# Alternating column order in the products of three stages of a hybrid decoder layer

## What is computed

```python
def s5_branch(u, ...):
    ...
    v = jax.nn.gelu(y).astype(u.dtype) @ w_glu          # 2048 x 4096
    v1, v2 = jnp.split(v, 2, axis=-1)
    return v1 * jax.nn.sigmoid(v2), ...

def mixer(h, ...):
    proj = h @ lp['w_in']
    ...
    merged = jax.nn.sigmoid(g_a) * y_a + jax.nn.sigmoid(g_b) * y_b
    return merged @ lp['w_out'], ...                    # 2048 x 2048

def swiglu(h, w_up, w_down):
    g, v = jnp.split(h @ w_up, 2, axis=-1)              # 2048 x 11264
    return (jax.nn.silu(g) * v) @ w_down                # 5632 x 2048
```

## Time and profile before

| | |
|---|---|
| median of 3 runs | 2365.61 us (2365.05 to 2366.68) |
| the profiled execution: its time, its span | 2365.34 us, 2363.6 us |
| mean granted TensorE clock | 1.000 |
| matmuls, share of the span in which TensorE is busy | 19158, 100% |
| VectorE, ScalarE, GpSimd busy | 70%, 45%, 5% |
| HBM traffic | 191 GB/s over the span |

### The profile page before, as it was taken

How to read it: one execution, slowest core, us unless ns; L and a number is a source line. 1 busy time by engine, 2 the same in 40 slices (tenths; PEclk the granted TensorE clock), 3 DMA queues, 4 the chain that set the end, 5 groups by cost and what they waited for, 6 DMA issues and landing times.

```text
span 2363.6 us, 49376 instructions
## 1 busy us (share of the span) xinstructions
PE 2355.7 (100%) x19158; PEld 2306.1 (98%) x19158; DVE 1653.1 (70%) x2923; ACT 1058.7 (45%) x1567; POOL 109.2 (5%) x202
## 2 busy tenths in 40 slices
PE   9999999999999999999999999999999999999999
PEld 9999999999999999999999999999999999999998
DVE  7798988989888877798956555765555555544444
ACT  6453544535445345545643333553343334333333
POOL 1000000000000002100400000000000000000000
PEclk9999999999999999999999999999999999999999
DMA  7676766677576678465977765555555555565543
GB/s 211 201 222 208 241 197 207 217 215 237 188 219 208 217 242 229 145 185 170 247 202 199 205 195 197 180 170 158 173 160 160 171 161 165 169 200 166 168 160 117
DMA packets 546112, 453.93 MB, mean 192 GB/s; under 512 B 31185, under 2 KB 520113, under 8 KB 545409
## 3 DMA queue, kind: packets, MB, share of 16 engines
q1 hardware_dynamic: 525936, 406.23, 57.3%
q0 software_dynamic: 13392, 34.33, 4.6%
q10 hardware_dynamic: 6624, 11.18, 1.4%
HBM read 412.01 MB, written 38.81 MB: 191 GB/s over the span
## 4 chain that ended last, share of the span: by engine, by line
PE 97%; DVE 2%; issue 0%; ACT 0%; POOL 0%; DVEq 0%; ACTq 0%; POOLq 0%
PE acc L2093 30%; PE acc L2094 29%; PE acc L2095 29%; PE side L2080 1%; PE side L2179 1%; PE side L2231 1%; PE side L2103 0%; PE side L2366 0%; DVE cacc L1336 0%; PE side L2397 0%; PE side L2379 0%; PE side L2213 0%; PE acc L2578 0%; PE side L2578 0%; PE side L2577 0%
## 5 line engine op out<-in xcount | busy, mean ns | idle before, releaser
L1291 DVE TENSOR_TENSOR w_lo<-raw,w_hi 128x1024 fp32r<-128x1024 f32 (+2 forms) x692 | 830.4, 1207 | 501.0 <-ACT w_hi L792 495.8
L792 ACT ACTIVATE w_hi<-raw 128x1024 fp32r<-128x1024 f32 (+2 forms) x692 | 716.7, 1045 | 864.4 <-PE acc L2095 834.2
L2093 PE MATMUL acc<-h_hi,w_hi 128*128 128x288 f32 x3344 | 1000.6, 299 | 0.0
L2095 PE MATMUL acc<-h_hi,w_lo 128*128 128x288 f32 x3344 | 987.0, 295 | 0.0
L2094 PE MATMUL acc<-h_lo,w_hi 128*128 128x288 f32 x3344 | 986.1, 295 | 0.0
L2093 PEld LDWEIGHTS acc<-h_hi,w_hi 128*128 128x128 f32 x3344 | 628.3, 188 | 17.1 <-issue 14.8
L2094 PEld LDWEIGHTS acc<-h_lo,w_hi 128*128 128x128 f32 x3344 | 628.0, 188 | 2.1 <-issue 2.1
L2095 PEld LDWEIGHTS acc<-h_hi,w_lo 128*128 128x128 f32 x3344 | 628.3, 188 | 0.0
L2093 PE MATMUL acc<-f_hi,w_hi 128*128 128x288 f32 x698 | 207.0, 297 | 0.0
L2095 PE MATMUL acc<-f_hi,w_lo 128*128 128x288 f32 x698 | 205.9, 295 | 0.0
L2094 PE MATMUL acc<-f_lo,w_hi 128*128 128x288 f32 x698 | 205.6, 294 | 0.0
(11 more groups left out here) (407 smaller groups left out, 2683.0 us busy)
## 6 DMA issues: line engine op xcount, KB each, us to landing
raw<-in_w_in_dram SPq DMA_DIRECT2D x512, 256.0 KB, 3.5
raw<-in_w_ffn_up_dram SPq DMA_DIRECT2D x352, 256.0 KB, 3.4
raw<-in_w_ffn_down_dram SPq DMA_DIRECT2D x160, 256.0 KB, 2.9
raw<-in_w_ssm_out_dram SPq DMA_DIRECT2D x128, 256.0 KB, 3.4
raw<-in_w_glu_dram SPq DMA_DIRECT2D x128, 256.0 KB, 3.7
h<-in_state_ssm_dram SPq DMA_DIRECT2D x32, 512.0 KB, 7.0
out_ssm_sample_dram<-h POOLq DMA_DIRECT2D x32, 512.0 KB, 4.0
raw<-in_w_out_dram SPq DMA_DIRECT2D x64, 256.0 KB, 3.1
```

Source lines behind the costliest of these rows:

```text
L792: copy = lambda out, in_, **k: nc.scalar.activation(out, in_, ACT.Copy, **k)
L1291: tt(w_lo[:, slot, 0:n], raw[:, slot, 0:n], w_hi[:, slot, 0:n].bitcast(F32), ALU.subtract).then_inc(lo_ready, 1)
L2093: mm(o_, wh, xh[:, kt, :], start=first and i == 0, stop=False)
L2095: done = mm(o_, wl, xh[:, kt, :], start=False, stop=last and i == n - 1)
```

## The change

The four operands of the three stages' products are read, and the accumulator written, in another order of the 288 columns: `in_runs` takes the row as two halves of 144 columns, cuts each half into runs of `run` columns, and goes through first run of the first half, first run of the second half, second run of the first half, and so on. Reading and writing use the same order, so column t of the operand still goes to column t of the accumulator. `run` is 16 in GLU (9 runs a half), 8 in the output projection (18 runs a half), 48 in FFN up (3 runs a half), and 0 (no reordering) everywhere else. Beside that, `base` goes up by 64 bytes, and `st5` is laid on a multiple of 128 in place of 32, by which it moves down 96 bytes. After this `w_hi`, `w_lo`, `h_hi`, `h_lo`, `y_hi`, `y_lo`, `f_hi`, `f_lo`, `v_hi`, `v_lo`, `mg_hi` and `mg_lo` all begin at 128 modulo 256.

```diff
--- before.py
+++ after.py
@@ -181,7 +181,7 @@
     u_dram = nc.dram_tensor("u_scratch", (D_MODEL, DL * NK), F32, kind="Internal").ap()
     y5_dram = nc.dram_tensor("y5_scratch", (D_MODEL, DL * NK), F32, kind="Internal").ap()
 
-    base = 16512
+    base = 16576
     top = nc.sbuf_usable_end
     used = {}
 
@@ -291,7 +291,7 @@
     ct5, at = sb("ct5", [P, 2, PAIRS, S5C], F32, at)
     pq5, at = sb("pq5", [P, 2, DL - 1, PAIRS], F32, at)
     gth, _ = sb("gth", [P, 2, T], F32, used["tm5"][1])
-    st5, at = sb("st5", [P, 72, 2, PAIRS], F32, top // 32 * 32 - 72 * 2 * PAIRS * 4)
+    st5, at = sb("st5", [P, 72, 2, PAIRS], F32, top // 128 * 128 - 72 * 2 * PAIRS * 4)
     assert used["st5"][0] >= used["pq5"][1] and used["pq5"][1] >= used["abc"][0]
     assert used["gth"][1] <= used["en5"][0]
     assert used["st5"][0] + 64 * 2 * PAIRS * 4 >= used["h0"][0]
@@ -2079,7 +2079,11 @@
                 k = in_.shape[0]
                 return pe.transpose(out, in_, ident[0:k, 0:k])
 
-            def chunk(c, slot, pair, xh, xl, tiles, first, last, width=2 * P, split=None, between=None):
+            def in_runs(v, run):
+
+                return v.rearrange("p (h c x) -> p c h x", h=2, x=run) if run else v
+
+            def chunk(c, slot, pair, xh, xl, tiles, first, last, width=2 * P, split=None, between=None, run=0):
 
                 pe.wait_ge(lo_ready, c + 1)
                 n = len(tiles)
@@ -2087,12 +2091,12 @@
                     if split is not None:
                         pe.wait_ge(sem("y_split"), split + i)
                     for m in range(width // P):
-                        o_ = acc[2 * pair + m][:, 0:T]
+                        o_ = in_runs(acc[2 * pair + m][:, 0:T], run)
                         at_ = i * width + m * P
                         wh, wl = w_hi[:, slot, at_:at_ + P], w_lo[:, slot, at_:at_ + P]
-                        mm(o_, wh, xh[:, kt, :], start=first and i == 0, stop=False)
-                        mm(o_, wh, xl[:, kt, :], start=False, stop=False)
-                        done = mm(o_, wl, xh[:, kt, :], start=False, stop=last and i == n - 1)
+                        mm(o_, wh, in_runs(xh[:, kt, :], run), start=first and i == 0, stop=False)
+                        mm(o_, wh, in_runs(xl[:, kt, :], run), start=False, stop=False)
+                        done = mm(o_, wl, in_runs(xh[:, kt, :], run), start=False, stop=last and i == n - 1)
                     if between:
                         between(i)
                 done.then_inc(multiplied, 1)
@@ -2304,12 +2308,12 @@
                     group_chunk(t, 7, 1)
                 side_work(t, 7, 1, True, False)
 
-            def outgroup(k, c0, pair, xh, xl, ready=None):
+            def outgroup(k, c0, pair, xh, xl, ready=None, run=0):
 
                 for kc in range(4):
                     if ready:
                         pe.wait_ge(*reach(ready, 4 * kc + 4))
-                    chunk(k * 4 + (c0 + kc), kc, pair, xh, xl, range(4 * kc, 4 * kc + 4), kc == 0, kc == 3)
+                    chunk(k * 4 + (c0 + kc), kc, pair, xh, xl, range(4 * kc, 4 * kc + 4), kc == 0, kc == 3, run=run)
 
 
             def q_turn(i):
@@ -2454,7 +2458,7 @@
                 if isinstance(k, int) and k < 2:
                     pe.wait_ge(*reach("gate_tanh", 30 + 2 * k))
                 wait(pe, "acc_freed", k - 1)
-                outgroup(k, C_GLU, (129 + b) % 2, v_hi, v_lo, ready)
+                outgroup(k, C_GLU, (129 + b) % 2, v_hi, v_lo, ready, run=16)
 
             glu(0, 0, "v_ready")
             glu(1, 1)
@@ -2527,7 +2531,7 @@
                         pe.wait_ge(lo_ready, C_UP)
                         closing((145 + b) % 2, kc, mg_hi, mg_lo, range(12, 16), msq, "m_squared", "m_summed", lambda: hold(3, acc[2]))
                     else:
-                        chunk(k * 4 + (C_OUT + kc), kc, (145 + b) % 2, mg_hi, mg_lo, range(4 * kc, 4 * kc + 4), kc == 0, kc == 3)
+                        chunk(k * 4 + (C_OUT + kc), kc, (145 + b) % 2, mg_hi, mg_lo, range(4 * kc, 4 * kc + 4), kc == 0, kc == 3, run=8)
 
             proj(0, 0)
             proj(1, 1)
@@ -2592,7 +2596,7 @@
                 else:
                     pe.wait_ge(freed, k + 23)
                 for kc in range(4):
-                    chunk(k * 4 + (C_UP + kc), kc, (153 + b) % 2, h_hi, h_lo, range(4 * kc, 4 * kc + 4), kc == 0, kc == 3)
+                    chunk(k * 4 + (C_UP + kc), kc, (153 + b) % 2, h_hi, h_lo, range(4 * kc, 4 * kc + 4), kc == 0, kc == 3, run=48)
                     if isinstance(k, int) and k == 4 and kc == 0:
                         x1_sums()
                     if isinstance(k, int) and k == 4 and kc == 1:
```

## The result

The changed kernel takes 2369.32 us (median of 18 runs, 2368.47 to 2370.39) against 2365.53 us for the kernel before (18 runs, 2364.78 to 2366.68): a ratio of 1.0016, 95% interval 1.0009 to 1.0022. It is slower by 3.8 us, where a gain of 10.9 us was forecast.

What follows compares the result with a forecast made beforehand. The prediction took TensorE, busy throughout, as the bound: products times start-to-start interval. Alignment 1.1 us plus column order 9.8 us gave 10.9 us gained, 2354.7 us; the forecast's own range was 2340 to 2360, the full range 2320 to 2382.

Steps and rivals of the forecast that it cites:

- The bound: Whole kernel: TensorE never waits, so time is number of products times the interval from one start to the next.
- Part 1: Alignment of operands in GLU and output projection: interval from 133.3 to 132.8 ns, 1.1 us gained.
- Part 2: Column order in GLU, output projection and FFN up: 6120 products at 131.2 ns, 9.8 us gained after the alignment.
- the two placements: Moving tiles' addresses modulo 256 alternate by 128; read from FFN down chunks as 131 and 134 ns a product.
- even tiles: FFN down tiles at the better placement, read as 131.2 ns a product and assumed for every reordered product.
- The rival of the jumps: Reordered products in three stages: each jump breaks TensorE's reads or accumulator writes, 0.42 ns each; 2394 us; chance 0.2.
- Neutral: Reordered products: column order changes nothing, only the alignment's 1.1 us is gained; 2364.5 us; chance 0.27.
- Nearly all of the loss goes: Reordered products: moving stream and weights no longer meet; up to 73 us gained, 2293 us; chance 0.13.
- Its best end: Reordered products: only the half-rate products' 1 ns stays lost, thus 121 ns; up to 73 us gained.
- the half-rate products: Plain f32 products of 288 columns: 0.241 us apiece against 240 ns, so only 1 ns lost, weight load included.
- The 13 ns: Each 288-column product: loss over the columns' 120.0 ns, taken to hang on moving addresses against those of weights being loaded.

Runs made afterwards that it cites:

- e3: Changed kernel with the accumulator written in plain order, only reads by runs: 135.6 ns in GLU, 136.6 in output projection, 132.2 in FFN up.
- e7: Changed kernel in plain order, each stage's products reading one place, 0, 32, 64 or 96 bytes past the weights' modulo 256: 133.3 ns at 32, 131.7 at the others.
- e8: Changed kernel in plain order, each stage's products reading one place, 128, 160, 192 or 224 bytes past the weights' modulo 256: 133.3 ns at all four.
- e4: Changed kernel with the moving operand read in plain order, only the accumulator written by runs: 132.8 ns in GLU, output projection and FFN up.

## Why the prediction was wrong

**The bound** was right: TensorE's interval sets the time in the three stages, and what they lose and gain comes through to the end (3.8 us of 3.8). **Part 1** was right in mechanism and size: 132.8 ns in GLU and output projection, 2364.46 us measured against 2364.5 for that part alone, and the stages whose relation stayed kept their 132.8.

**Part 2 is the step that failed.** It took "the nearest row, the better of the two placements", for all 6120 products: "if that gives every product what even tiles have, 131.2 ns". Measured: 135.6, 136.7 and 132.2 ns. A gain of 9.8 us was put in where the order loses 3.8 + 1.1 = 4.9 us against plain order with the new alignment. The rows did show that the interval hangs on places, and experiment e3 confirms that the reads matter, and e7 and e8 speak for the place; the rows did not show which way a mixture goes. Nor is 131.2 ns the price of a placement: it is an even tile's part of two tiles that take 1593 ns together, and in GLU, with the alignment alone, both tiles have 132.8. Picking the better of two levels for a stream that visits both was a choice without a row, and the argument that alternating halves slows the stream through the low address bits, which is truest for short runs, failed worst there: runs of 8 on halves are the slowest of all. One of the three stages, FFN up, went the forecast way, by 0.6 ns of the 1.6.

**The rival of the jumps** had the sign right, though its 2394 us are 25 too many, and its mark, mg_hi over v_hi over h_hi, is exactly what the changed profile shows. It is wrong all the same: the price is not in the writes (e4), not in the number of jumps (72 against 8, halves against thirds). At a fixed price it would not fit either: 3.9 ns for 35 jumps, 2.8 for 17, a gain for 5. The statement of the Trainium skill that any non-contiguous accumulator pattern slows matmuls significantly (PSUM — Partial Sum Buffer, "Specifications (TRN2)") doesn't hold here for runs of 8 columns and more: writes by runs alone left 132.8 ns. **Neutral** came nearest in the number, 2364.5 us against 2369.32, and the result lies within the 4.7 us that were counted as no change. That is luck: its sign, 132.8 ns everywhere, is refuted in all three stages, and two losses and a gain happened to leave 3.8 us. **Nearly all of the loss goes** was wrong by far: no order or place tried came under 131.1 ns. Its best end also rests on a wrong 1 ns: the half-rate products start 242.4 ns apart by the ns starts (243, 241, 243), 2.4 over their 240, which the 0.01 us of the row can't tell.

The 13 ns also contradict the reading that I gave them: I took the half-rate rows as a sign that they are the meeting of two streams, but with a half of the weight load they fell by 1.5 ns and with a quarter by 1.1. That weight loads take nothing from a running product (the Trainium skill, TensorE: Matmul & The Clock Gate, "Part 2: What happens when you issue a matmul") is thus nearer to the truth in plain order than I made it, 1.1 to 1.5 ns a product off. Whether the 3 to 4 ns that runs of 16 and 8 on halves add would go with a shorter load wasn't tried.

## What to carry to other kernels

Where TensorE is never idle, read the interval from first and last start, not the duration, and compute change by count times interval: here that closes to 0.1 us. An order of reads is worth trying when the interval differs between placements, but no row of the plain kernel tells the sign; one profiled kernel with another run in each stage does. Take a second profile before a place or a run is named as the cause, and compare all times of a kernel and not its median alone: two patterns can hide in them. And a loss that rises with the number of pieces is no proof that the pieces cost: change where they lead and keep their number.

## What was not expected of the hardware

- Products of 288 fp32r columns follow each other 11 to 17 ns over the columns' time at 2.4 GHz (12.8 in plain order, 12.2 and 11.7 at 272 and 256 columns), and a half or a quarter of the weight load takes only 1.5 or 1.1 ns off.
- The intervals come in steps of 0.56 ns: 24 products take a whole multiple of 13.3 ns.
- Reading the same 288 columns in another order moves the interval from 131.1 to 136.7 ns; writing them in another order doesn't move it.
- A cause that five profiles agreed on (the place modulo 512) fell at the second profile of one of the kernels: intervals of 132.2 and 133.3 ns are both stable over a whole stage of one program, and in the gate stage both occur in one execution, with a change only at a break in the stream.
